# A hybrid decoder trunk on one Trainium2 core: other loads, squares and sums at the beginning of its first layer

## The reference

```python
def rms_norm(x, g, eps=RMS_EPS):
    xf = x.astype(jnp.float32)
    y = xf * lax.rsqrt(jnp.mean(xf * xf, axis=-1, keepdims=True) + eps)
    return (y * g.astype(jnp.float32)).astype(x.dtype)

def reference(x, norm_g, ...):
    for i in range(DEPTH):
        h = rms_norm(x, norm_g[i])
        ...
        x = x + y          # y = mixer(h, weights of layer i)
    return x
```

## Time and profile before

| | us |
|---|---|
| median of 3 runs | 1822.09 |
| lowest and highest | 1820.61, 1824.07 |
| profiled execution | 1820.88 |
| its span, first to last instruction | 1819.1 |

### The profile page before, as it was taken

How to read it: one execution, slowest core, us unless ns; L and a number is a source line. 1 busy time by engine, 2 the same in 40 slices (tenths; PEclk the granted TensorE clock), 3 DMA queues, 4 the chain that set the end, 5 groups by cost and what they waited for, 6 DMA issues and landing times.

```text
span 1819.1 us, 22598 instructions
## 1 busy us (share of the span) xinstructions
PE 1767.8 (97%) x8872; PEld 1431.8 (79%) x8872; DVE 851.8 (47%) x1294; ACT 824.9 (45%) x1191; POOL 550.3 (30%) x143
## 2 busy tenths in 40 slices
PE   7999999999999999999999999999999999999999
PEld 5688789878898666668878888888877887887787
DVE  6765954242142555544643444441277577434410
ACT  6575343685233666644422222222266734338721
POOL 1333320333424000024344444444334234104443
PEclk9999999999999999999999999999999999999999
DMA  4223210222222010112223222222222132012222
GB/s 171 93 70 93 77 39 17 78 93 93 93 93 93 24 47 27 44 47 96 90 94 104 101 92 92 92 98 96 96 84 81 69 102 74 12 47 93 92 94 69
DMA packets 48775, 143.69 MB, mean 79 GB/s; under 512 B 28080, under 2 KB 30256, under 8 KB 32816
## 3 DMA queue, kind: packets, MB, share of 16 engines
q1 hardware_dynamic: 48688, 142.50, 22.9%
HBM read 137.25 MB, written 5.24 MB: 78 GB/s over the span
## 4 chain that ended last, share of the span: by engine, by line
PE 71%; issue 17%; POOL 4%; DVE 4%; ACT 4%; DMA 0%; POOLq 0%; SPq 0%; DVEq 0%; ACTq 0%
PE ps L1565 18%; PE ps L1567 18%; PE ps L1566 18%; POOL w_lo L441 4%; PE ps L1828 2%; PE ps L1884 2%; PE ps L1855 1%; PE ps L2030 1%; PE ps L1870 1%; PE ps L1879 1%; PE ps L2045 1%; PE ps L1839 1%; PE ps L2003 1%; ACT w_hi L531 1%; PE ps L1950 1%
## 5 line engine op out<-in xcount | busy, mean ns | idle before, releaser
L441 POOL TENSOR_TENSOR w_lo<-w_raw,w_hi 128x2048 fp32r<-128x2048 f32 x107 | 497.2, 4646 | 1054.1 <-ACT w_hi L531 842.1
L1565 PE MATMUL ps<-h_hi,w_hi 128*128 128x512 f32 x1488 | 604.3, 406 | 21.8 <-DVE w_lo L959 10.0
L1567 PE MATMUL ps<-h_hi,w_lo 128*128 128x512 f32 x1488 | 581.7, 391 | 0.0
L1566 PE MATMUL ps<-h_lo,w_hi 128*128 128x512 f32 x1488 | 581.3, 391 | 0.0
L1565 PEld LDWEIGHTS ps<-h_hi,w_hi 128*128 128x128 f32 x1488 | 280.4, 188 | 105.0 <-issue 28.9
L1566 PEld LDWEIGHTS ps<-h_lo,w_hi 128*128 128x128 f32 x1488 | 280.6, 189 | 59.5 <-issue 5.5
L1567 PEld LDWEIGHTS ps<-h_hi,w_lo 128*128 128x128 f32 x1488 | 280.2, 188 | 59.6
L531 ACT ACTIVATE w_hi<-w_raw 128x2048 fp32r<-128x2048 f32 (+1 forms) x126 | 238.7, 1894 | 129.1 <-PE ps L1567 123.8
L1565 PE MATMUL ps<-y_hi,w_hi 128*128 128x512 f32 x448 | 174.3, 389 | 0.0
L1566 PE MATMUL ps<-y_lo,w_hi 128*128 128x512 f32 x448 | 174.3, 389 | 0.0
L1567 PE MATMUL ps<-y_hi,w_lo 128*128 128x512 f32 x448 | 174.3, 389 | 0.0
(11 more groups left out here) (190 smaller groups left out, 2285.7 us busy)
## 6 DMA issues: line engine op xcount, KB each, us to landing
w_raw<-w_tiles SPq DMA_DIRECT2D x124, 1024.0 KB, 4.9
x<-x_t SPq DMA_DIRECT2D x4, 512.0 KB, 6.8
out_t<-x SPq DMA_DIRECT2D x8, 256.0 KB, 5.7
w_raw<-w_tiles SPq DMA_DIRECT2D x2, 512.0 KB, 5.0
scr_u<-lt SPq DMA_DIRECT2D x8, 128.0 KB, 2.7
u_blk<-scr_u SPq DMA_DIRECT2D x2, 512.0 KB, 3.3
scr_v<-v_blk SPq DMA_DIRECT2D x2, 512.0 KB, 2.6
scr_t<-v_t SPq DMA_DIRECT2D x2, 512.0 KB, 3.6
```

What stands on the lines that cost most here:

```text
L441: pool.tensor_tensor(w_lo[:, slot, :], w_raw[:, slot, :], w_hi[:, slot, :].bitcast(F32), ALU.subtract).then_inc(lo_done, 1)
L1565: pe.matmul(out_, w_h, m_h, start=start, stop=False)
L1566: pe.matmul(out_, w_h, m_l, start=False, stop=False)
L1567: return pe.matmul(out_, w_l, m_h, start=False, stop=stop)
```

## The change

x is loaded in five pieces instead of four, the first two of one block each. The weights of tile 1 are loaded ahead of both constant tables instead of between them. All eight first squares are made on ScalarE: block 0's ahead of `hi(0)`, blocks 1 and 2 behind the last rounding, then `hi(1)`, then the other five. VectorE makes no squares, and adds blocks 1 and 2 to block 0 ahead of `low_w(1)`, and 4 to 3 and 6 to 5 behind it. So four sums are left for TensorE. They no longer stand in and behind tile 0, but in a row inside tile 1, behind its third block (k = 2).

```diff
+X_LOADS = ((0, 1), (1, 2), (2, 4), (4, 6), (6, 8))
...
         sp.dma_start(par[:, :], params).then_inc(par_loaded, 16)
-        for m in range(KD // 2):
-            sp.dma_start(x[:, 2 * m:2 * m + 2, :], x_in[:, 2 * m:2 * m + 2, :]).then_inc(x_loaded[m], 16)
-            if m == 0:
+        for n, (m0, m1) in enumerate(X_LOADS):
+            sp.dma_start(x[:, m0:m1, :], x_in[:, m0:m1, :]).then_inc(x_loaded[n], 16)
+            if n == 0:
                 sp.dma_start(w_part(w_raw, 0), tiles[0].rearrange("p (k n) -> p k n", n=2 * P)[:, :, 0:P]).then_inc(raw[0], 16)
+        sp.dma_start(w_raw[:, 1, :], tiles[1]).then_inc(raw[1], 16)
         sp.dma_start(cf[:, :], const_f).then_inc(loaded, 16)
-        sp.dma_start(w_raw[:, 1, :], tiles[1]).then_inc(raw[1], 16)
         sp.dma_start(cb[:, :], const_b).then_inc(loaded, 16)
...
-            hi(t0 + 1)
+            if l:
+                hi(t0 + 1)
...
+        def square_first(m):
+            act.activation(sq8[:, m, :], x[:, m, :], ACT.Square).then_inc(sq0_done, 1)
         for m in range(KD):
-            act.wait_ge(x_loaded[m // 2], 16)
+            act.wait_ge(x_loaded[x_load(m)], 16)
             round_x(0, m)
-            if m % 2 == 0:
-                act.activation(sq8[:, m, :], x[:, m, :], ACT.Square).then_inc(sq0_even, 1)
             if m == 0:
+                square_first(0)
                 hi(0)
+        square_first(1)
+        square_first(2)
+        hi(1)
+        for m in range(3, KD):
+            square_first(m)
...
-            if m % 2:
-                dve.tensor_tensor(sq8[:, m, :], x[:, m, :], x[:, m, :], ALU.mult).then_inc(sq0_odd, 1)
-            if m in (1, 3):
-                dve.wait_ge(sq0_even, m // 2 + 1)
-                dve.wait_ge(sq0_odd, m // 2 + 1)
-                dve.tensor_tensor(sq8[:, m - 1, :], sq8[:, m - 1, :], sq8[:, m, :], ALU.add).then_inc(sq0_pair, 1)
+        def add_first(to, m):
+            dve.wait_ge(sq0_done, m + 1)
+            dve.tensor_tensor(sq8[:, to, :], sq8[:, to, :], sq8[:, m, :], ALU.add).then_inc(sq0_added, 1)
+        add_first(0, 1)
+        dve.wait_ge(sq0_added, 1)
+        add_first(0, 2)
         low_w(1)
+        add_first(3, 4)
+        add_first(5, 6)
...
-        def sum_first(m):
-            ...
-            mm = pe.matmul(ps[7][:, :], ones, sq8[:, m, :], start=(m == 0), stop=(m == KD - 1))
+        def sum_first():
+            pe.wait_ge(loaded, 32)
+            pe.wait_ge(sq0_done, KD)
+            for n, m in enumerate((0, 3, 5, 7)):
+                pe.wait_ge(sq0_added, (2, 3, 4, 4)[n])
+                mm = pe.matmul(ps[7][:, :], ones, sq8[:, m, :], start=(m == 0), stop=(m == KD - 1))
+            mm.then_inc(ss_done, 1)
...
-                if l == 0 and k >= 4:
-                    sum_first((0, 2, 4, 5)[k - 4])
                 if l and k == 3:
                     sum_x(l)
-            if l == 0:
-                for m in (6, 7):
-                    sum_first(m)
             ready(t0 + 1)
             for k in range(KD):
                 ...
+                if k == 2 and l == 0:
+                    sum_first()
```

More of the change, by code:

```diff
@@ L74, in y_at, with x_load @@
     return (c + 8) % 16
+X_LOADS = ((0, 1), (1, 2), (2, 4), (4, 6), (6, 8))
+def x_load(m):
+    return next(n for n, (m0, m1) in enumerate(X_LOADS) if m0 <= m < m1)
 PHASE1 = 10
@@ L304, in trunk @@
     par_loaded, loaded = sem("params_loaded"), sem("const_loaded")
-    x_loaded = [sem(f"x_loaded{m}") for m in range(KD // 2)]
+    x_loaded = [sem(f"x_loaded{m}") for m in range(1 + KD // 2)]
     raw = [sem("raw0_loaded"), sem("raw1_loaded")]
@@ L310, in trunk @@
     sq_done, sum_done = sem("x_sq_done"), sem("x_sum_done")
-    sq0_even, sq0_odd = sem("first_sq_act"), sem("first_sq_dve")
-    sq0_pair = sem("first_sq_pair")
+    sq0_done = sem("first_sq_done")
+    sq0_added = sem("first_sq_added")
     ss_done = sem("x_ss_done")
@@ L1544, in _ @@
         for m in range(KD):
-            dve.wait_ge(x_loaded[m // 2], 16)
+            dve.wait_ge(x_loaded[x_load(m)], 16)
             low_x(0, m)
@@ L1594, in sum_x @@
             pe.matmul(ps[7][:, :], ones, sq[:, (KD - 1) % 2, :], start=False, stop=True).then_inc(ss_done, 1)
-        def sum_first(m):
[L1598 to L1603, removed]
-            mm = pe.matmul(ps[7][:, :], ones, sq8[:, m, :], start=(m == 0), stop=(m == KD - 1))
-            if m == KD - 1:
-                mm.then_inc(ss_done, 1)
+        def sum_first():
[5 more added lines that the diff above has]
+            mm.then_inc(ss_done, 1)
         def in_part(t, c, k, start, stop):
```

## The result

The changed kernel takes 1825.53 us (median of 20 runs, 1823.07 to 1829.26), the kernel before 1821.01 (20 runs, 1819.84 to 1824.07). The ratio is 1.0023, with a 95% interval of 1.0017 to 1.0029: **slower by 0.23%**, some 4.2 us (3.1 to 5.3). The forecast was 1824.8 us, inside its range of 1820.6 to 1827.4. Its shift of 2.7 us had the right sign and was some 1.5 us too small. That the time itself came within 0.7 us of the forecast is in part luck: the prediction started from a median of three runs, 1822.09, and 20 runs have it at 1821.01. The forecast gave 0.62 to a change of less than 0.2% and 0.32 to a larger loss; the measured 0.23% lies just beyond that line, with its interval on both sides of it.

A forecast was written before the change was run, and what follows sets the result against it. The prediction took VectorE's chain behind the first layer's row norm (rstd) as the bound, with TensorE setting the long run. Ln +2.4 and clock +0.3 gave +2.7 us on the 1822.09 median: 1824.8 us, range 1820.6 to 1827.4.

The forecast's parts named there:

- the Ln decides: First layer: when the row norm's sum is ready sets the time; Ln 2.4 us later, at 26.05 instead of 23.69.
- The rival without rstd on the path: TensorE alone sets the time up to 46 us, so tile 1's 1.7 us are gained: 1820.4 us; chance 0.10.
- TensorE's terms: Tile 1 from 18.3: 18 matmuls take 4.1 us, four sums 3.45, and the Ln starts 0.20 later, at 26.05.
- the start of `hi(1)`: ScalarE, tile 1: free at 13.9 after the squares, starts at 14.0 when the weights land, instead of 14.88.
- the k sum of head 7: First layer, TensorE: its matmul, at 81.81 before, comes near 84.5, with the PE stream as before from there.
- the prediction's own sign of a fault in the clock or the landing: First layer: an Ln later than 27 us means the clock or the weights' landing is at fault.
- the forecast's 0.8: Tile 1's weights, no longer behind the table's 0.36 MB, land 0.8 us earlier, at 14.0.
- The bounds that the prediction set for the small rows: Two x loads with 2 KB rows: between nothing and 0.4 us lost; nothing taken, 0.4 kept for the range.
- The rival in which the weights come no earlier: Small x rows cost what the table gave back; `hi(1)` stays at 14.88, shift +3.6, 1825.7 us; chance 0.09.
- The rival with the clock: The clock falls in the wait between tiles 0 and 1; rstd another 1.7 us later, +4.4, 1826.5 us; chance 0.13.
- The forecast of 0.3 us: Half clock for 3.4 us behind the wait ahead of tile 3 costs 1.7 us; later waits absorb all but 0.3.
- The rule beside the rows: TensorE's clock: half rate is the array's default, which only activity lifts; trace agrees at 912.22, not at 210.79.

The follow-up runs named there:

- before, again: The unchanged kernel before, run once more for a second profiled execution: 1824.30 us.
- changed, again: The changed kernel itself, run once more for a second profiled execution: 1829.81 us.
- changed, third: The changed kernel itself, run a third time for a profiled execution: 1824.79 us.
- sum behind k = 0: The changed kernel with its four sums behind tile 1's first block instead of its third: 1822.92 us against 1821.24, ratio 1.0010.
- late rstd: The kernel before with five copies of the sum on ScalarE, each waited for, ahead of the first layer's Ln: 1825.19 us against 1821.24, ratio 1.0020.
- sums between the tiles: The changed kernel with all squares and additions ahead of hi(1) and low_w(1), four sums between tiles 0 and 1: 1819.08 us against 1821.63, ratio 0.9984.

## Why the prediction was right, and where its sizes were off

**What sets the time.** The claim was that the Ln decides, not the end of tile 1. The distance from the Ln to tile 3's first matmul is the best witness:

| execution | Ln | tile 3 | distance |
|---|---|---|---|
| before | 23.69 | 46.17 | 22.48 |
| before, again | 24.17 | 46.65 | 22.48 |
| changed | 27.87 | 50.35 | 22.48 |
| changed, again | 28.60 | 51.08 | 22.48 |
| changed, third | 26.28 | 48.76 | 22.48 |
| sum behind k = 0 | 23.62 | 46.11 | 22.49 |
| late rstd | 27.01 | 49.49 | 22.48 |
| sums between the tiles | 21.23 | 43.72 | 22.49 |

It is the same within 0.01 us, wherever tile 1 stands, and 22.48 to 22.50 in the six other profiled executions. The same holds further on: GpSimd's sixth low part comes 80.25 to 80.28 us behind the Ln in 12 of the 14 executions; the two others are those with 6.8 us at half clock ahead of it. The late-rstd run shows that it is a cause and not only a companion, and the chain behind it has no slack. The rival without rstd on the path is refuted by the same run.

**TensorE's terms.** 18 matmuls and four sums were put at 7.55 us, the Ln at 7.75 us behind the start of tile 1. Measured: 27.87 - 20.00 = 7.87 and 26.28 - 18.42 = 7.86. Tile 0's start was put at 9.35 and came at 9.29. Tile 2 waits for `low_w(2)` in each of the three, by 1.4 us (forecast 1.5). Tile 0's slow stretch, which the prediction counts as eleven matmuls, is ten: ten starts lie from 10.00 up to the one at 14.60. So tile 0 was put 0.2 us too short, which the sum of the prediction doesn't use.

**The term that was mis-sized is the start of `hi(1)`**, put at 14.0. In the third execution it came at 14.12, and there everything is as written down: Ln at 26.28 (forecast 26.05), tile 3 at 48.76 (48.6), the k sum of head 7 near 84.45 (84.5). In the other two it came at 15.70 and 14.86. An Ln later than 27 us was the prediction's own sign of a fault in the clock or the landing. Two of the three executions show it: the first by the landing, the second by the clock.

The prediction let ScalarE be free at 13.9 because the last pair of x was the last to arrive. That path is wrong. ScalarE still has earlier blocks to round by then. From its start on blocks 2 and 3 (at 9.13, 9.85 or 10.64 in the three executions), six roundings and two squares, 5.0 us, follow without a gap. That the wrong path gave a fitting number is luck, since in the kernel before these blocks had landed at 8.9, and 8.9 + 5.0 is 13.9 too. The weights are bound to the same event. In the nine executions with the new loads they land 4.9 to 5.1 us behind blocks 2 and 3 (landed at 8.9 to 10.6), in the five with the old loads 5.9 to 6.0 us (landed at 8.8 to 10.2). So taking the table out from between is worth 0.9 us, close to the forecast's 0.8. What varies, and has a mean 0.2 us later with the new loads (9.55 against 9.36), is when blocks 2 and 3 are there. The squares' end and the weights' landing lie within 0.2 us of each other in all three executions, so no run tells which of the two holds `hi(1)`; both come late when those blocks do. `hi(1)` has a mean of 14.9 in the three. The bounds that the prediction set for the small rows, nothing lost and 0.4 us lost, were too narrow: the landings of one and the same program differ by 1.6 us. The rival in which the weights come no earlier has its number, 14.88, in the second execution, but not its cause.

**The clock.** The rival with the clock had a chance of 0.13 and came true in one of three executions. Its price, 1.7 us, is close to the measured one: 9.5 us from `low_w(1)` to the Ln instead of 7.9. Its chance isn't refuted by this: of the 20 runs of the changed kernel two have as low a mean granted clock and as long a time (0.994, 1829.25 and 1829.26 us) as that execution (0.994, 1829.81). In the three, the Ln is 2.6, 4.2 and 4.9 us behind 23.69, mean 3.9 (3.7 against the mean of both executions of before).

Behind the wait ahead of tile 3 the clock fell each time, once for 3.4 us and twice for 6.8. The forecast of 0.3 us was for a fall of 3.4 us, and this one costs nothing. The third execution lost nothing by it (shift 2.59 at tile 3, and 2.59 at GpSimd's sixth low part, 106.54 against 103.95), and neither did the kernel before with the late rstd (3.32 and 3.31). The falls of 6.8 us cost 0.85 in the first and 1.0 in the second (4.91, then 109.87 - 103.95 = 5.92). So the term's reason was right, that waits absorb a part. Its length and what a short fall leaves were not, and the mean of 0.6 is twice the forecast. Measured from the mean of both executions of the kernel before, 3.7 and 0.6 make 4.3 us, against 4.2 (3.1 to 5.3) by the ratio. With three executions and two, so close an agreement is partly chance.

**The rule beside the rows.** The Trainium skill, TensorE: Matmul & The Clock Gate, section "What's actually happening", has the gate set "based on how busy the PE has been recently". The execution with the 2.62 us wait agrees. The prediction counted the short wait at 210.79 against the rule; the section doesn't say that each wait brings half rate back, so neither that one nor those of 0.82 and 2.00 us ahead of tile 1, behind which the clock held, speak against it.

**What stays open.** The sum behind k = 0 measured 1.8 us above the kernel before (0.2 to 3.5), though in its trace the Ln is as early as before. Its profiled execution is the fastest of its 11 runs (1821.12, mean granted clock 0.999); the slowest had 1826.25 and 0.996, and the mean is 0.9975 where the kernel before has 0.9984. In its runs 0.001 of clock goes with 1.3 us, so an estimate from these numbers gives 1.3 us to half clock, and 0.4 to weights that land at 14.6 in the mean instead of 14.2. Where those falls lie its one profile doesn't show. Why blocks 2 and 3 land anywhere between 8.8 and 10.6 us, and tile 1's weights with them, wasn't tried.

## What to carry to other kernels

When work is reordered, find the value that the next stage's longest chain begins with, here rstd, and ask of each move whether it comes ahead of that value or behind it. The change took two sums away from ahead of it and put 18 matmuls there. The same parts with the sums in the wait between the tiles gain 0.16% against the kernel before, where the change loses 0.23%. And where a step hangs on a landing in the first microseconds, its time is a spread and not a number: TensorE's own work ahead of the sum hid it in the kernel before, and the change exposed it.

## What the runs showed of the hardware that was not expected

The landings vary by themselves: tile 1's weights, in 14 profiled executions, between 14.0 and 16.2 us, and in the first execution of the changed kernel they landed 0.4 us after the table that was issued behind them (15.7 against 15.3). In that execution the order of issue was not the order of landing. The spread arises ahead of blocks 2 and 3 of x, within the first 11 us; from their landing to that of tile 1's weights it is 4.9 to 5.1 us in each execution with the new loads. A wait of 2.00 us ahead of tile 1 was followed by a granted clock of 1.00 and one of 2.62 us by 0.50. The length of one wait doesn't decide it: in the first execution of the changed kernel a wait of 2.44 us at 920.23 was followed by full clock, where the kernel before fell to 0.52 behind 2.17 us at 912.22. Behind the wait of 3.1 us ahead of tile 3 the clock was at half for 3.4 us in one execution of the changed kernel and for 6.8 in two. The kernel before with the late rstd and the changed kernel with the old loads have the same wait, and had 3.4 us.
